# Norm factors of memory, queries and keys as powers on GpSimd, and rotation tables in four products, in the first mixing stage of a two-block decoder kernel

## The reference, cut to what matters

```python
z = h @ w_in[l]
x_rnn, g_rnn, q, k, v, gate_a, gate_b = jnp.split(z, SPLIT_IDX, axis=-1)
xc = _causal_conv(x_rnn, conv_w[l], conv_b[l])
hr = _rg_lru(xc, ...)
y_a = (hr * jax.nn.gelu(g_rnn)) @ w_rnn_proj[l]
...
q = _rope(_rmsnorm(q.reshape(B, S, N_Q_HEADS, HEAD_DIM), q_gain), cos, sin)
k = _rope(_rmsnorm(k.reshape(B, S, N_KV_HEADS, HEAD_DIM), k_gain), cos, sin)
```

## Time and profile before

| what | value |
|---|---|
| median of 3 runs | 957.69 us (956.09 to 958.09) |
| the profiled execution's own time | 957.8 us |
| span in the profile | 955.9 us |
| busy share of the span: PE, PEld, DVE, ACT, POOL | 99%, 80%, 56%, 49%, 0% |

### The profile page before, as it was taken

The page is one execution under the profiler, slowest core; times in us unless marked ns, Lnnn a source line. Parts: engine busy times, 40 slices in busy tenths (PEclk is TensorE's granted clock), DMA queues, the critical chain, the costliest instruction groups (busy, mean ns, idle before and its releaser), DMA issues.

```text
span 955.9 us, 14085 instructions
## 1 busy us (share of the span) xinstructions
PE 941.7 (99%) x5793; PEld 761.9 (80%) x5793; DVE 535.5 (56%) x848; ACT 471.4 (49%) x733; POOL 4.2 (0%) x13
## 2 busy tenths in 40 slices
PE   9999999999999999999999999999999999999996
PEld 8989787887889999999889887889876575756553
DVE  5888896766666556555586875676453212122214
ACT  5488665767444444544567756445452121313113
POOL 0000000000000000000000000000000000000000
PEclk9999999999999999999999999999999999999998
DMA  9944465434555555554645734476757999999992
GB/s 319 299 148 153 158 234 204 134 131 152 171 185 197 200 176 177 177 178 144 214 153 174 232 129 155 154 248 237 270 198 287 409 408 408 409 409 409 409 409 97
DMA packets 89861, 223.55 MB, mean 234 GB/s; under 512 B 9161, under 2 KB 14018, under 8 KB 89794
## 3 DMA queue, kind: packets, MB, share of 16 engines
q1 hardware_dynamic: 87488, 219.62, 64.3%
q10 hardware_dynamic: 2306, 2.99, 0.9%
HBM read 221.54 MB, written 1.05 MB: 233 GB/s over the span
## 4 chain that ended last, share of the span: by engine, by line
PE 85%; DVE 6%; ACT 3%; issue 2%; DMA 2%; SPq 1%; ACTq 0%; DVEq 0%
PE pb L492 18%; PE pb L494 18%; PE pb L493 18%; PE pb L2510 12%; PE pb L2533 6%; PE pb L2550 3%; PE pb L2476 2%; DMA raw<-in_w_in 2%; DVE wl L1565 2%; PE pb L582 2%; ACT wh L1015 1%; PE pb L662 1%; PE pb L650 1%; PE pb L726 1%; PE pb L633 1%
## 5 line engine op out<-in xcount | busy, mean ns | idle before, releaser
L1565 DVE TENSOR_TENSOR wl<-raw,wh 128x2048 fp32r<-128x2048 f32 (+3 forms) x112 | 246.4, 2208 | 95.8 <-ACT wh L1015 95.5
L1015 ACT ACTIVATE wh<-raw 128x2048 fp32r<-128x2048 f32 (+3 forms) x112 | 206.7, 1852 | 109.1 <-PE pb L494 98.8
L492 PE MATMUL pb<-wh,th 128*128 128x512 f32 (+2 forms) x620 | 246.3, 397 | 0.5 <-DVE wl L1565 0.2
L494 PE MATMUL pb<-wh,tl 128*128 128x512 f32 (+2 forms) x620 | 238.9, 385 | 0.0
L493 PE MATMUL pb<-wl,th 128*128 128x512 f32 (+2 forms) x620 | 238.6, 385 | 0.0
L492 PE MATMUL pb<-th,wh 128*128 128x256 f32 x528 | 152.6, 289 | 0.4 <-DVE wl L1565 0.4
L494 PE MATMUL pb<-th,wl 128*128 128x256 f32 x528 | 149.3, 283 | 0.0
L493 PE MATMUL pb<-tl,wh 128*128 128x256 f32 x528 | 149.3, 283 | 0.0
L492 PEld LDWEIGHTS pb<-wh,th 128*128 128x128 f32 x620 | 116.5, 188 | 25.3 <-DVE wl L1565 2.5
L494 PEld LDWEIGHTS pb<-wh,tl 128*128 128x128 f32 x620 | 116.4, 188 | 23.4
L493 PEld LDWEIGHTS pb<-wl,th 128*128 128x128 f32 x620 | 116.7, 188 | 20.6
(11 more groups left out here) (415 smaller groups left out, 1124.5 us busy)
## 6 DMA issues: line engine op xcount, KB each, us to landing
raw<-in_w_in SPq DMA_DIRECT2D x31, 1024.0 KB, 5.3
raw<-in_w_up SPq DMA_DIRECT2D x16, 1024.0 KB, 5.6
raw<-in_w_down SPq DMA_DIRECT2D x16, 1024.0 KB, 5.3
raw<-in_w_exp_gate SPq DMA_DIRECT2D x9, 1024.0 KB, 17.2
raw<-in_w_xkv SPq DMA_DIRECT2D x8, 1024.0 KB, 5.1
raw<-in_w_exp_down SPq DMA_DIRECT2D x8, 1024.0 KB, 16.9
raw<-in_w_exp_up SPq DMA_DIRECT2D x7, 1024.0 KB, 13.8
my<-in_w_exp_down SPq DMA_DIRECT2D x7, 1024.0 KB, 14.2
```

The lines of the kernel that those rows point to most:

```text
L492: PE.matmul(o, lh, rh, start=start, stop=False, skip_group_check=True)
L494: return PE.matmul(o, ll, rh, start=False, stop=stop, skip_group_check=True)
L1015: ACTE.activation(hi_of(i), raw_of(i), ACT.Copy).then_inc(S["hi"], 1)
L1565: DVE.tensor_tensor(lo_of(i), raw_of(i), hi_of(i).bitcast(F), ALU.subtract).then_inc(S["lo"], 1)
```

## The change

Three edits, all in the first mixing stage.

1. The rotation tables: in place of eight products of 128x64, four products of 128x128. Each multiplies one table (cosine or sine), repeated for both halves, by a whole gain. The tables lie in another order in `TB`, and the rotation picks them by the index (0, 3, 1, 2). The semaphore `tables` counts four instead of one.
2. The memory factors: POOL waits for the memory's squares, multiplies by 1/1024 and adds the epsilon, and raises the 128x2 tile to the power -0.5. DVE's 13 instructions go.
3. The query and key factors: POOL waits for the third `sums`, adds 64 times the epsilon to the 128x40 tile, raises it to the power -0.5 (which gives the factor divided by 8, as the attention wants it for the queries), and multiplies the key part by 8. DVE's 13 instructions (12 and the copy `rq8`) go. DVE waits for `rq` at 2 before it scales the keys.

```diff
@@ pool_main
             POOL.memset(least, 2.0 ** -100).then_inc(S["xr0"], 1)
+            POOL.memset(exponent, -0.5).then_inc(S["powers"], 1)
             POOL.memset(XR[:, :, 0:3], 0.0).then_inc(S["xr0"], 1)
+            POOL.wait_ge(S["square"], SQ["mem"] + 2)
+            POOL.tensor_scalar(mrs, ssq["mem"], 1.0 / D, EPS, ALU.mult, ALU.add).then_inc(S["powers"], 1)
+            POOL.wait_ge(S["powers"], 2)
+            POOL.tensor_tensor(mrs, mrs, exponent.to_broadcast([128, 2]), ALU.pow).then_inc(S["mem_rs"], 1)
+            POOL.wait_ge(S["qk_sum"], 3)
+            POOL.tensor_scalar(rqk, rqk, 1.0, 64 * EPS, ALU.mult, ALU.add).then_inc(S["powers"], 1)
+            POOL.wait_ge(S["powers"], 3)
+            POOL.tensor_tensor(rqk, rqk, exponent.to_broadcast([128, 40]), ALU.pow).then_inc(S["rq"], 1)
+            POOL.wait_ge(S["rq"], 1)
+            POOL.tensor_scalar(rk, rk, 8.0, None, ALU.mult).then_inc(S["rq"], 1)
             POOL.wait_ge(S["turn_lo"], TB_["mem"] + 8)
@@ dve_rope
-                DVE.wait_ge(S["tables"], 1)
+                DVE.wait_ge(S["tables"], 4)
...
-                    tb = TB[:, f0 + i].unsqueeze(2).to_broadcast([128, 2, nh, 32])
+                    tb = TB[:, f0 + (0, 3, 1, 2)[i]].unsqueeze(2).to_broadcast([128, 2, nh, 32])
@@ dve_main
-            f = 0
-            for g in (gq, gk):
-                for tab, hf_ in ((cosv, 0), (sinv, 1), (cosv, 1), (sinv, 0)):
-                    ins = DVE.tensor_tensor(TB[:, f], tab, g[:, 32 * hf_:32 * hf_ + 32].unsqueeze(1).to_broadcast([128, 2, 32]), ALU.mult)
-                    if f == 7:
-                        ins.then_inc(S["tables"], 1)
-                    f += 1
+            for n, g in enumerate((gq, gk)):
+                for i, tab in enumerate((cosv, sinv)):
+                    halves = g.rearrange("p (f n) -> p f n", f=2).unsqueeze(2).to_broadcast([128, 2, 2, 32])
+                    DVE.tensor_tensor(TB[:, 4 * n + 2 * i:4 * n + 2 * i + 2], tab.unsqueeze(1).to_broadcast([128, 2, 2, 32]), halves,
+                                      ALU.mult).then_inc(S["tables"], 1)
             dve_then(DVE.tensor_scalar(nsnk, snk, -1.0, None, ALU.mult))
-            DVE.wait_ge(S["square"], SQ["mem"] + 2)
-            dve_rsqrt(mrs, [(ssq["mem"], D)], last="mem_rs")
...
             sums(2)
-            DVE.wait_ge(S["qk_sum"], 3)
-            dve_rsqrt(rqk, [(rqk, 64)])
-            dve_after()
-            DVE.tensor_scalar(rq8, rq, 0.125, None, ALU.mult).then_inc(S["rq"], 1)
             dve_unit("g", 1, 1)
             dve_gelu_in(0)
+            DVE.wait_ge(S["rq"], 2)
             DVE.tensor_tensor(rope_args(2)[0], rope_args(2)[0], rk.rearrange("p (t h) -> p t h", t=2).unsqueeze(3).to_broadcast([128, 2, 4, 64]),
                               ALU.mult).then_inc(S["k_scaled"], 1)
```

More of the change, by code:

```diff
@@ L147 @@
      "cols_mm", "cols", "lam", "lam_exp", "xr0", "mem_rs", "xc0", "xc", "gate_mm", "gate_a", "rnn_u", "rnn_m", "rnn_root",
-     "gelu_sq", "gelu_q", "gelu_t", "gelu", "scan", "rnn_y", "y_hi", "y_lo", "tables", "qk_sq", "qk_sum", "rq", "k_scaled",
+     "gelu_sq", "gelu_q", "gelu_t", "gelu", "scan", "rnn_y", "y_hi", "y_lo", "tables", "qk_sq", "qk_sum", "rq", "k_scaled", "powers",
      "rope_d", "rope", "mem_scaled", "kq_mm", "kq_T", "sc_mm", "sc_add", "negmax", "expd", "sk", "sk_exp",
@@ L288, in build @@
         mrs = small(2)
-        rqk, rq8 = small(40), small(32)
+        rqk, exponent = small(40), small(1)
         rq, rk = rqk[:, 0:32], rqk[:, 32:40]
@@ L1127, in act_exps @@
                     ACTE.activation(sl, sl, ACT.Exp, bias=w["nm"][:, 4 * t + i:4 * t + i + 1],
-                                    scale=SC2 if n >= 4 else rq8[:, 16 * t + h:16 * t + h + 1],
+                                    scale=SC2 if n >= 4 else rq[:, 16 * t + h:16 * t + h + 1],
                                     accum_out=w["dn"][:, 4 * t + i:4 * t + i + 1]).then_inc(S["expd"], 1)
@@ L1757, in dve_max @@
             m3, nm3, sk3 = by_tile(mx), by_tile(nm), by_tile(w["sk"])
-            dve_then(DVE.scalar_tensor_tensor(m3, m3, -1.0, by_tile(rq8)[:, :, h0:h0 + 4], ALU.mult, ALU.mult))
+            dve_then(DVE.scalar_tensor_tensor(m3, m3, -1.0, by_tile(rq)[:, :, h0:h0 + 4], ALU.mult, ALU.mult))
             dve_after()
```

## The result

The changed kernel takes 958.98 us (median of 10 runs, 957.74 to 960.43) against 957.18 us for the kernel before, measured beside it (10 runs, 955.63 to 958.15): ratio 1.0025, 95% interval [1.0017, 1.0033]. It is slower, by 1.8 us between the medians and by 2.4 us by that ratio; 4.9 us faster were forecast. The profiled execution has a span of 958.5 us.

A forecast was written before the change was run, and what follows sets the result against it. PE, busy 99% of the span, was taken as the bound, waiting 5.1 us for DVE early on; less 0.2 us kept, 4.9 us off 957.8 gave 952.9 us, own range 952.0 to 953.8, 951.6 to 955.9 with two rivals.

The forecast's parts named there:

- T: Time of POOL's three query/key instructions with handovers: 1.9 us taken, 0.9 to 3.0 as bounds, 2.8 us of it hidden.
- Query and key factors: DVE's chain from 98.51 to 101.37 us goes to POOL: later wl passes come 2.9 us earlier, 4.9 in all.
- the first rival: POOL's key chain is shut out by DVE's two-input passes, so DVE waits 1.3 to 1.9 us: 954.4 us, chance 0.24.
- The third rival: POOL's power before the key scaling is slow, column by column at 0.3 us each: slower, 962 us, chance 0.09.
- Tables: Rotation tables on DVE: four products for eight save 0.3 us, bounds 0 and 0.6, counted as nothing.
- Memory factors: DVE's 13 steps before the loop, 2.62 us, go; ACT's first convolution limits the loop's move to 2.0 us.
- What PE can win: PE's eight waits for DVE between 36 and 130 us add up to 5.1 us, of which 0.2 stays.
- so the sum holds for it too: The 4.9 us gain from the profiled execution, 957.8 us, also applies to the runs' median, 957.69, only 0.1 below.
- No change given back later: PE is busy 575.73 of 576 us from 124 to 700 us, so everything behind keeps what PE gains by 124.
- The rule on shared ports: A two-SBUF-input DVE instruction and a GpSimd instruction reading SBUF exclude each other for a whole instruction, first to start first.
- The first-call cost: About 6 us for the first call to a freshly loaded GpSimd routine; the first, earlier POOL chain should have paid it.

The follow-up runs named there:

- keys and sums early: Changed kernel with the keys' sums of squares moved into the loop's last turn and POOL raising the 8 key columns first: 953.67 us, ratio 0.9971.
- sums early: Changed kernel with the keys' sums of squares moved up into the loop's last turn on DVE: 953.35 us, ratio 0.9968.
- keys first: Changed kernel with POOL raising the 8 key columns before the 32 query columns, DVE waiting for the keys alone: 953.70 us, ratio 0.9973.
- memory alone: Kernel before with only the memory factors moved to POOL, tables and query/key factors as before: 954.28 us, ratio 0.9977.
- wait first: Changed kernel with DVE's wait for the factors moved ahead of its wl pass and gelu step: 958.67 us, ratio 1.0034.
- query, key and tables: Changed kernel with the memory factors back on DVE, leaving query and key factors on POOL and the new tables: 960.87 us, ratio 1.0046.

## Why the prediction was wrong

The step that failed is T, in "Query and key factors": 1.9 us taken, 3.0 as the upper end, 10.0 measured. Of the 8.1 us between, 5.5 are the power: I took 1.2 us for 40 columns, with 2.3 as its bound, from the rate of POOL's product, and it takes 6.74, 0.16 us a column where the product takes 0.0023. Another 2.6 are the first short instruction, 2.80 us for the 0.2 taken: POOL was shut out by DVE's passes. This was the first rival, but priced with my own T, and I let the two add up nowhere.

Apart from the size of what PE can win (below), the sum's other steps held. The third rival, the slow power, said that the gain is gone at T = 7.7 us and each us more is lost: 10.0 - 7.7 = 2.3 us slower, and K is 2.26 us longer, the medians 1.8 and 2.4 slower in the two sets of runs. Only its price was off (0.3 us a column where it is 0.16, so T = 12.7), and its chance, 0.09, was far too low: no row showed a power, and the argument against it, that the product works in vectors, carried over from one operation to another.

Point by point:
- Tables: 0.28 us saved (1.17 to 0.89; 0.3 said), worth nothing beside the memory factors, as said: DVE stands in front of ACT's convolution, 1.53 us where it was 0.73.
- Memory factors: the loop moves by 2.1 us (2.0 said), up to ACT's limit, as said.
- What PE can win: read as 5.1 us from one execution's waits, it is 2.9 us in the medians. The four waits in the loop came from a late landing; with an early one they don't exist. The step that carried the sum from that execution to the median ("so the sum holds for it too") was wrong, although the median of the three runs known then lay only 0.1 us away: the 10 runs beside the changed kernel have 957.18, the later ones 956.29 to 956.50. Had T been hidden as forecast, the time would have come out 2.9 us lower and not 4.9: the forecast would have kept its sign but missed its size.
- No change given back later: right in all kernels, the medians move with K until PE's waits are used up:

```
kernel                      K us    K less 64.27   median less that of before
keys and sums early         59.06      -5.21          -2.6
sums early                  59.00      -5.27          -2.9
keys first                  61.10      -3.17          -2.6
memory alone                62.17      -2.10          -2.0
changed                     66.53      +2.26          +1.8, +2.4 (two sets)
wait first                  66.81      +2.54          +2.3
query, key and tables       68.41      +4.14          +4.5
```

- The rule on shared ports (the Trainium skill, "SBUF — State Buffer", "Who interferes with whom"): the trace agrees for the short instructions, 0.23 us alone and 2.80 beside two DVE passes. It differs for the power, which took 6.75 us beside such passes and 6.74 without, and left them at 2.29 us; there the measurement decides. What the runs show is that the power isn't excluded for its whole length, not that it never waits: that of 32 columns took 5.42 us where it was issued just before a pass (100.11 and 100.15) and 5.72 where it was issued in the middle of one (88.75, the passes from 88.50), in the kernel with both edits; each is one trace.
- The first-call cost (the Trainium skill, "GPSIMD Engine Reference", "Instruction dispatch"): the first power of the kernel, on two columns, took 0.86 us and followed the instruction ahead of it by 0.08 us; no such cost shows here.

## What to carry to other kernels

An operation that no row shows has no price: bound it by "unknown" and ask at which price the sign turns, or move its start so early that the price doesn't matter, which here turned 2.4 us lost into 2.9 us won with one call moved. Waits read from one execution may belong to that execution: if the chain behind them starts at a DMA's landing, ask how far the landing varies before counting them as gain. And a chain of twelve short VectorE steps of 0.2 us each is hard to beat by an engine that pays by the column: at 40 columns POOL's power alone took 6.74 us for VectorE's 2.9, at two columns its two steps took 1.2 for 2.6. Split off the columns that are needed first.

## What the runs showed of the hardware that was not expected

- A power on POOL costs about 0.4 us and 0.16 us for each column of 128 partitions: 0.70 to 0.86 us for 2 columns, 1.63 and 1.64 for 8, 5.42 and 5.72 for 32, 6.74 to 6.78 for 40 in all seven traces that have it. In six of these seven VectorE stood beside it, in one it worked (6.75).
- A short POOL instruction that reads SBUF waited out a two-input pass of VectorE that had just begun, and the second one issued right behind it (2.71 to 2.80 us for 0.23 in the six traces in which VectorE's passes ran ahead of it).
- The landing of one early unit varied by 2.0 us between executions (its rounding started at 37.93 to 39.91 us). Of the kernel before, the two profiled executions with 38.2 and 38.3 took 956.2 us, the one with 39.91 took 957.8; its runs lie within 2.5 us, those of the two kernels with early sums, in whose traces PE never waits for VectorE in this stretch, within 0.6 and 1.0 us.
- PE standing 4.66 us took the granted clock to 0.50, and 5.32 us in another kernel too; standing 3.10 us in another execution left it at 1.00.
